# A second attention whose transposes and value products stand ahead of the look-ahead scores in every step

## The chip, the core and the metric

The program runs on one core of one Trainium2 chip, as a single launch. The metric is the device time of the whole program in microseconds (us); the number used for a kernel is the median of its runs.

## What is computed

The input is a sequence of 512 tokens of width 1024, in fp32. Block one is a gated linear recurrence (RG-LRU) with its projections, followed by an attention layer with a sliding window. Block two has a mixer of three attention families that share a sequence of "groups", and an MLP behind it. Cut to what the change touches:

```
stick:  z = q k^T * scale ; a = exp(log_sigmoid(z) + sum of log_sigmoid(-z) over later keys) ; o = a v   # 6 heads
cmp:    softmax over 31 compressed keys, 4 heads at once                                                # 4 heads
sel, win: softmax(q k^T * scale - slope * distance) v, causal                                           # 4 heads each
dil:    softmax over three key strips with stride 1, 4 and 16, merged by their sums                     # 2 heads
x = x + concat(o) @ w_out ;  x = x + relu(norm(x) @ w_up)^2 @ w_down
```

## The kernel before

The tokens are cut into 4 blocks of 128 (`n`). A **group** is one head of one kind with one query block `n`; its key width `w` is 128, 256, 384 or 512. The second attention (`make_attention(2)`) has 68 groups, numbered `i` from 0 to 67, in an order written out by hand: stick heads mixed with cmp, sel and win heads first, the dil heads between the last sel and win ones (constant `LATE`, 24 groups).

Each engine walks over the same step number `i` in its own queue, and semaphores tie the four queues together. In step `i`:

- **PE** (TensorE) issues `scores(i + 4)` (L769 and L772; L762 for cmp), `turn(i)` (the transposes of the probabilities of group `i`, L785) and `values(i - 1)` (the products with V of group `i - 1`, L805). After these stand, in some steps, `pair_turn` and `turn_chunk` (further transposes, L827: of a finished pair of heads, or of a dilated query or key, named ("q", m) or ("k", m)), and in 24 steps up to 29 a `piece`: 12 matmuls of a projection (L1298 to L1300). The pieces belong to three projections G1, G2 and G3, each with 4 token tiles of 2 pieces.
- **ACT** (ScalarE) takes the scores of a stick group in four passes (L878, L881, L883, L885) in step `i` for group `i + 3`, exponentiates masked scores (L904; L897 for cmp) and finishes stick probabilities (L921) for group `i + 2`, copies odd chunks of transposes out of PSUM (L926), and takes dilated chunks (L946, L947).
- **DVE** (VectorE) masks the scores of the other kinds (L1039; L1018 for cmp) for group `i + 3`, runs the running sum and the subtraction of stick groups (L1053, L1054) for `i + 2`, copies even chunks (L973), and scales finished heads (L1114, L1119).
- **POOL** (GpSimd) splits every weight unit into a high and a low part (L1248, L1250, L1251) ahead of the matmuls that use it. Four units fit into the ring, and a unit is split only when the matmuls with its predecessor in that slot are done (L1247 is the first instruction after that wait). Behind the units of G3 it prepares and splits the dilated queries and keys (L1209, L1219).

What a PE block waits for: `scores(i + 4)` waits until the score bank (three of them, four from group 36 on) has been read; `turn(i)` waits for the probabilities of `i`, and for its chunk bank. The chunks, numbered in PE's order, alternate between PSUM banks 3 and 4, so a chunk waits until the chunk two before it has been copied out. `values(i - 1)` waits for the copies of its chunks, and at the start of a head for the finished head before it in its output bank.

Whether the scores of a step go in front or behind was decided by a flag `late`. It was set for the scores of the last 24 groups, that is in steps 40 to 63:

```
late = a == 2 and ng - len(LATE) <= ahead < ng
if 0 <= ahead < ng and not late:
    scores(ahead)
...
if late:
    scores(ahead)
```

Of the kernel before, what the change touches and what calls it, by code (L numbers as in the profile page):

```python
# [153 lines left out]
LATE = "nnDnDnnDnDnnDnDnnDnDnnnn"  # L154
# [145 lines left out]
def two_block_kernel(nc, x_d, weights_d, params_d, tables_d, swa_d, ident_d, out_d):  # L300
    BANK, FREE, BEFORE, LAST_USE = plan()
    ctx = ExitStack()
    with ctx:
# [263 lines left out]
        def make_attention(a):  # L567
# [37 lines left out]
            def strip_read(st):  # L605

                return s[f"read{SB.index(strip_bank[st])}_"], strip_count[st]

            s = att[a]
            ng = len(groups)  # L610
# [130 lines left out]
            def pe_part(pe, item, tail, behind_scores=None):  # L741
# [33 lines left out]
                def turn(i):  # L775
                    g = groups[i]
                    if i == 0 and a == 2:
                        for k in (3, 4):
                            pe.wait_ge(FREESEM[LAST_USE[k][0]], LAST_USE[k][1])
                    pe.wait_ge(*probs_ready(i))  # L780
                    for c, blocks in g["chunks"]:
                        if c >= 2:
                            pe.wait_ge(s[("pt_even", "pt_odd")[c % 2]], c // 2)
                        for j, (strip, _, kb) in enumerate(blocks):
                            mm = pe.transpose(B[3 + c % 2][:, j * P:(j + 1) * P], probs_of(i, strip)[:, kb * P:(kb + 1) * P], ident[:])  # L785
                        mm.then_inc(s["pt_ready"], 1)

                def values(i):
                    g = groups[i]
                    b = g["b"]  # L790
                    kind = batches[b]["kind"]
                    if i == start_of[b]:
                        if ahead_in_bank(b) is not None:
                            pe.wait_ge(*fin_of(ahead_in_bank(b)))
                        elif a == 2:
                            pe.wait_ge(FREESEM[LAST_USE[bank_of[b]][0]], LAST_USE[bank_of[b]][1])
                        if kind in ("stick", "dil"):
                            pe.wait_ge(evac_a, FREE[("G4" if kind == "stick" else "G3", 3)][1])
                    out = out_cols(b, g["n"], 4 * HD if kind == "cmp" else VW)
                    first, total = True, sum(len(bl) for _, bl in g["chunks"])  # L800
                    for c, blocks in g["chunks"]:
                        pe.wait_ge(s[("pt_even", "pt_odd")[c % 2]], c // 2 + 1)
                        for j, (s_, _, kb) in enumerate(blocks):
                            total -= 1
                            mm = pe.matmul(out, pt[:, c % slots, j * P:(j + 1) * P], value_ap(g, s_, kb),  # L805
                                           start=first, stop=total == 0)
                            first = False
                    mm.then_inc(s["o_done"], 1)

                def pair_turn(p):  # L810
                    for b, batch in enumerate(batches):
                        if batch["pair"] == pair_of[p] and (batch["last"] or batch["kind"] == "dil"):
                            pe.wait_ge(*fin_of(b))
                    if a == 1 and before7[("pair", p)]:
                        pe.wait_ge(*before7[("pair", p)])
                    if a == 2:
                        turn_chunk(("pair", p), otok[:, slot[p]])
                        return
                    for t in range(TB):
                        mm = pe.transpose(B[7][:, t * P:(t + 1) * P], otok[:, slot[p], t, :], ident[:])  # L820
                    mm.then_inc(s["pairT"], 1)

                def turn_chunk(key, src):
                    c = chunk_of[key]
                    pe.wait_ge(*chunk_taken(c - 2))
                    for t in range(TB):
                        mm = pe.transpose(B[3 + c % 2][:, t * P:(t + 1) * P], src[:, t, :], ident[:])  # L827
                    mm.then_inc(s["pt_ready"], 1)

                for i in range(-LOOK - 1, ng + OUT_LAG):  # L830
                    ahead = i + LOOK + 1
                    late = a == 2 and ng - len(LATE) <= ahead < ng
                    if 0 <= ahead < ng and not late:
                        scores(ahead)
                    if i == -2 and a == 2:
                        behind_scores()
                    if 0 <= i < ng:
                        turn(i)
                    if 0 <= i - V_LAG < ng:
                        values(i - V_LAG)  # L840
                    if late:
                        scores(ahead)
                    if i - TURN_LAG in pairs:
                        pair_turn(pairs.index(i - TURN_LAG))
                    if a == 2 and i in TURNS2:
                        k = DIL_ORDER.index(TURNS2[i])
                        pe.wait_ge(dil_doubled, k + 1)
                        turn_chunk(TURNS2[i], doubles[k % 2])
                    if i in part_at:
                        key, q, parts = part_at[i]  # L850
                        if q == 0 and before7[key]:
                            pe.wait_ge(*before7[key])
                        item(key, range(KD * q // parts, KD * (q + 1) // parts))
                    if a == 2 and i in PIECES:
                        item(*PIECES[i])
                    for m, k0, k1 in TAILS[a].get(i - ng, ()):
                        if k0 > 0:
                            pass
                        elif m < 3:
                            pe.wait_ge(*strip_read(max(st for st, k in enumerate(strip_bank) if k == m)))  # L860
                        else:
                            pe.wait_ge(s["pt_even"], last_chunk // 2 + 1)
                        tail(m, range(k0, k1))
# [306 lines left out]
            def pool_part(pool):  # L1170
# [51 lines left out]
                for k in range(len(DIL_ORDER) + 1):  # L1222
                    if k < len(DIL_ORDER):
                        double(k)
                    if k > 0:
                        split_dil(k - 1)

            return pe_part, act_part, dve_part, len(pairs), lambda p: chunk_taken(chunk_of["pair", p]), pool_part

        def slope10(i):  # L1230
# [1256 lines left out]
```

## Time and profile before

| what | value |
|---|---|
| median of 3 runs | 1145.09 us |
| lowest, highest | 1144.65, 1145.69 us |
| the profiled execution's own time | 1148.06 us |
| span of its trace, first to last instruction | 1146.0 us |
| mean granted TensorE clock | 0.992 |
| PE, DVE, ACT, POOL busy | 96%, 54%, 38%, 46% of the span |

The second attention, from its first scores to its last value products, lies between 557.9 and 757.2 us of the span. The steps that the diff touches, 0 to 39, run from 568.39 us (`scores(4)`) to 693.09 us, where `turn(40)` starts. Steps were found in the trace by counting matmuls: a `turn` has one L785 for each 128 keys, a `values` has two L805 for each (fp32 data, two passes), and `scores` of a stick group three L769 and one L772, of sel and win two L769.

### The profile page before, as it was taken

The numbers are of one execution on the slowest core, as the hardware profiler recorded it, in microseconds if no ns is written. First come the engines' busy times: TensorE is split into PE (matmuls) and PEld (weight loads), VectorE is DVE, ScalarE is ACT, GpSimd is POOL, SyncE is SP. The second block draws the span as 40 slices with busy tenths as digits, with TensorE's granted clock in tenths as the row PEclk, the third lists the DMA queues.
The fourth block names the chain that finished last, engine by engine and source line by source line (L and its number), as shares of the span: only waits on it lengthen the run. The fifth ranks groups of instructions, "written<-read, shape, count | busy, mean of one in ns | idle before, by whom it ended". The sixth has DMA issues, their size and how long they took to land.

```text
span 1146.0 us, 16131 instructions
## 1 busy us (share of the span) xinstructions
PE 1101.0 (96%) x5801; PEld 940.1 (82%) x5801; DVE 619.3 (54%) x1102; ACT 435.5 (38%) x890; POOL 523.6 (46%) x521
## 2 busy tenths in 40 slices
PE   6999999999989999999999887999999999999998
PEld 5788888888869998888798886888878888888887
DVE  6869686668556763656655547856521321321321
ACT  5364758453335661213565578522110200210210
POOL 0000000000352434979833647229956776776772
PEclk9999999999999999999999989999999999999999
DMA  6332322313220101333311200103423222322221
GB/s 251 114 107 76 127 90 95 128 56 113 92 90 19 37 21 36 112 100 122 121 34 50 74 1 20 56 19 111 129 74 105 97 92 94 103 96 92 93 91 53
DMA packets 27279, 97.18 MB, mean 85 GB/s; under 512 B 3024, under 2 KB 3408, under 8 KB 27088
## 3 DMA queue, kind: packets, MB, share of 16 engines
q1 hardware_dynamic: 27216, 96.32, 25.1%
q8 instruction: 41, 0.67, 0.2%
q14 instruction: 22, 0.18, 0.0%
HBM read 94.21 MB, written 2.10 MB: 84 GB/s over the span
## 4 chain that ended last, share of the span: by engine, by line
PE 70%; DVE 9%; issue 8%; POOL 6%; ACT 6%; DMA 1%; POOLq 0%; SPq 0%; DVEq 0%; ACTq 0%
PE bank L1298 20%; PE bank L1300 20%; PE bank L1299 20%; PE bank L805 4%; PE bank L769 3%; POOL wl L1251 3%; PE bank L785 2%; POOL wh L1248 2%; DVE arena L2026 1%; DVE wl L1977 1%; ACT wh L1657 1%; POOL wl L1250 1%; DMA x<-x_in 1%; POOL hold L1247 1%; DVE arena L2361 0%
## 5 line engine op out<-in xcount | busy, mean ns | idle before, releaser
L1247 POOL TENSOR_TENSOR hold<-hold 128x2 f32<-128x2 f32 x117 | 29.9, 256 | 521.4 <-PE bank L1300 521.4
L1298 PE MATMUL bank<-xh,wh 128*128 128x512 f32 x568 | 227.1, 400 | 11.9 <-DVE xl L1946 9.8
L1299 PE MATMUL bank<-xl,wh 128*128 128x512 f32 x568 | 222.7, 392 | 0.0
L1300 PE MATMUL bank<-xh,wl 128*128 128x512 f32 x568 | 222.7, 392 | 0.0
L1298 PE MATMUL bank<-yh,wh 128*128 128x512 f32 x520 | 204.1, 393 | 2.9 <-DVE yl L2366 2.4
L1299 PE MATMUL bank<-yl,wh 128*128 128x512 f32 x520 | 203.0, 390 | 0.0
L1300 PE MATMUL bank<-yh,wl 128*128 128x512 f32 x520 | 203.0, 390 | 0.0
L1251 POOL TENSOR_TENSOR wl<-raw,wh 128x512 fp32r<-128x512 f32 x117 | 173.7, 1484 | 0.0
L1250 POOL TENSOR_TENSOR wl<-raw,wh 128x512 fp32r<-128x512 f32 x117 | 158.5, 1355 | 9.8
L1298 PEld LDWEIGHTS bank<-xh,wh 128*128 128x128 f32 x568 | 107.5, 189 | 35.2 <-issue 12.1
L1300 PEld LDWEIGHTS bank<-xh,wl 128*128 128x128 f32 x568 | 107.6, 189 | 22.8
L1248 POOL TENSOR_SCALAR wh<-raw 128x1024 fp32r<-128x1024 f32 x117 | 125.8, 1075 | 0.0
L1299 PEld LDWEIGHTS bank<-xl,wh 128*128 128x128 f32 x568 | 107.6, 189 | 21.6 <-issue 0.7
L1298 PEld LDWEIGHTS bank<-yh,wh 128*128 128x128 f32 x520 | 97.9, 188 | 24.7 <-DVE yl L2366 3.3
L1300 PEld LDWEIGHTS bank<-yh,wl 128*128 128x128 f32 x520 | 98.0, 189 | 20.6
L1299 PEld LDWEIGHTS bank<-yl,wh 128*128 128x128 f32 x520 | 98.1, 189 | 20.1
L1910 ACT ACTIVATE arena<-arena 128x512 f32<-128x512 f32 x32 | 20.3, 633 | 246.4 <-DVE arena L2361 246.4
L2373 DVE TENSOR_TENSOR x<-bank,x 128x512 f32<-128x512 f32 x32 | 22.1, 692 | 142.4 <-PE bank L1300 142.4
L805 PE MATMUL bank<-arena 128*128 128x64 f32 (+1 forms) x620 | 87.3, 270 | 3.2 <-ACT arena L926 2.4
L1977 DVE TENSOR_TENSOR wl<-raw,wh 128x1024 fp32r<-128x1024 f32 x56 | 68.0, 1222 | 39.8 <-ACT wh L1657 39.4
L1298 PE MATMUL bank<-wh,xh 128*128 128x512 f32 (+2 forms) x224 | 84.3, 376 | 4.1 <-POOL wl L1251 3.0
L805 PEld LDWEIGHTS bank<-arena 128*128 128x128 f32 x620 | 82.0, 196 | 6.0 <-ACT arena L926 2.9
(258 smaller groups left out, 1801.0 us busy)
## 6 DMA issues: line engine op xcount, KB each, us to landing
raw<-weight_units SPq DMA_DIRECT2D x173, 512.0 KB, 3.5
x<-x_in SPq DMA_DIRECT2D x4, 512.0 KB, 8.0
out_fm<-x SPq DMA_DIRECT2D x8, 256.0 KB, 2.0
arena<-tables SPq DMA_DIRECT2D x1, 1024.0 KB, 10.3
par<-params SPq DMA_DIRECT2D x1, 166.0 KB, 2.3
arena<-swa_table SPq DMA_DIRECT2D x1, 128.0 KB, 11.1
ident<-identity SPq DMA_DIRECT2D x1, 64.0 KB, 8.3
```

Of the source, the lines that this page charges most:

```text
L769: mm = pe.matmul(out, q, kk, start=t == 0, stop=t == len(terms) - 1 and kind != "stick")
L785: mm = pe.transpose(B[3 + c % 2][:, j * P:(j + 1) * P], probs_of(i, strip)[:, kb * P:(kb + 1) * P], ident[:])
L805: mm = pe.matmul(out, pt[:, c % slots, j * P:(j + 1) * P], value_ap(g, s_, kb), start=first, stop=total == 0)
L1247: pool.tensor_tensor(hold[:], hold[:], hold[:], ALU.add).then_inc(held, 1)
L1248: pool.tensor_scalar(wh[:, j, :], raw[:, j, :], 1.0, 1.0, ALU.mult, ALU.mult).then_inc(high_done, 1)
L1250: pool.tensor_tensor(wl[:, j, 0:512], raw[:, j, 0:512], wh[:, j, 0:512], ALU.subtract)
L1251: pool.tensor_tensor(wl[:, j, 512:1024], raw[:, j, 512:1024], wh[:, j, 512:1024], ALU.subtract)\
L1298: pe.matmul(out, lh, rh, start=start, stop=False)
L1299: pe.matmul(out, lh, rl, start=False, stop=False)
L1300: return pe.matmul(out, ll, rh, start=False, stop=stop)
L1977: dve.tensor_tensor(wl[:, u % RING, :], raw[:, u % RING, :], wh[:, u % RING, :], ALU.subtract)\
L2373: dve.tensor_tensor(x[:, m, :], B[4 + m % 4][:], x[:, m, :], ALU.add).then_inc(down_read, 1)
```

## The change

The flag is now set in every step from 0 on. In steps 0 to 39 the scores, those of groups 4 to 43, move behind `turn(i)` and `values(i - 1)`. They stay ahead of `pair_turn`, of `turn_chunk` and of the piece. Steps 40 to 63 had this order already. Nothing is added or taken out, and no other queue changes.

```
--- before.py
+++ after.py
@@ -829,7 +829,7 @@
 
                 for i in range(-LOOK - 1, ng + OUT_LAG):
                     ahead = i + LOOK + 1
-                    late = a == 2 and ng - len(LATE) <= ahead < ng
+                    late = a == 2 and 0 <= i and ahead < ng
                     if 0 <= ahead < ng and not late:
                         scores(ahead)
                     if i == -2 and a == 2:
```

## Rows read from the trace of the kernel before

**Rows 1.** First line of the page.

```profile
span 1146.0 us, 16131 instructions
```

**Rows 2.** Stages: start:end length, then PE, PEld, DVE, ACT, POOL busy; clock, DMA, GB/s.

```profile
568.40:592.20 23.80, 23.64 (x158) 23.37 (x159) 15.21 (x43) 18.36 (x53) 2.38 (x3) 1.00 0.08 24
592.20:608.80 16.60, 14.90 (x105) 14.12 (x103) 9.50 (x38) 10.20 (x43) 16.18 (x16) 1.00 0.29 95
608.80:626.60 17.80, 16.93 (x107) 16.29 (x108) 9.17 (x26) 10.00 (x28) 0.02 (x1) 1.00 0.10 32
626.60:643.70 17.10, 14.14 (x94) 12.71 (x92) 11.16 (x22) 8.25 (x22) 16.77 (x17) 1.00 0.28 92
643.70:667.40 23.70, 23.67 (x149) 23.34 (x150) 7.34 (x24) 10.12 (x29) 4.17 (x10) 0.93 0.07 23
667.40:693.10 25.70, 20.04 (x133) 18.17 (x132) 14.74 (x34) 22.37 (x56) 16.82 (x14) 0.87 0.00 1
693.10:757.40 64.30, 56.95 (x451) 52.22 (x449) 47.76 (x146) 38.83 (x114) 25.09 (x25) 1.00 0.11 34
```

**Rows 3.** Waits in 520 to 660 us: total, times, longest.

```profile
POOL hold L1247 <- PE bank L1300: 40.0, 3, 21.4
```

**Rows 4.** PE by line and form, 568.4 to 693.1 us; behind the bar its idle time.

```profile
L805 PE MATMUL bank<-arena 128*128 128x64 f32 x168 | 24.6, 278 | 2.4 <-ACT arena L926 2.0 <-DVE arena L1119 0.3
L1298 PE MATMUL bank<-wh,xh 128*128 128x384 f32 x64 | 23.7, 371 | 3.9 <-POOL wl L1251 3.0 <-ACT arena L1888 0.9
...
L785 PE MATMUL bank<-ident,arena 128*128 128x128 f32 x91 | 18.6, 298 | 2.7 <-ACT arena L947 2.0 <-DVE yl L1144 0.7
```

**Rows 5.** PE's timeline in steps 12, 30 and 39: start, duration; idle in brackets.

```profile
606.22 0.66 PE L805 MATMUL bank<-arena 128*128 128x64 f32 x4 [1.30 <-ACT arena L926]
...
667.25 0.39 PE L769 MATMUL bank<-yh 128*128 128x512 f32 x1
...
667.95 0.22 PE L772 MATMUL bank<-yh 128*128 128x128 f32 x1
668.91 0.30 PE L785 MATMUL bank<-ident,arena 128*128 128x128 f32 x1 [0.75 <-ACT arena L947]
669.59 0.66 PE L805 MATMUL bank<-arena 128*128 128x64 f32 x4 [0.37 <-ACT arena L926]
670.08 1.05 PE L827 MATMUL bank<-ident,arena 128*128 128x128 f32 x8
...
689.13 0.48 PE L769 MATMUL bank<-yh 128*128 128x512 f32 x1
...
691.37 0.41 PE L785 MATMUL bank<-ident,arena 128*128 128x128 f32 x2 [1.24 <-ACT arena L947]
692.15 0.66 PE L805 MATMUL bank<-arena 128*128 128x64 f32 x4 [0.37 <-ACT arena L926]
692.64 0.61 PE L827 MATMUL bank<-ident,arena 128*128 128x128 f32 x4
```

**Rows 6.** POOL's timeline in step 12: the last unit of G2.

```profile
606.78 1.94 POOL L1251 TENSOR_TENSOR wl<-raw,wh 128x512 fp32r<-128x512 f32 x1
```

**Rows 7.** ACT's timeline in its steps 31, 37 and 40.

```profile
670.29 0.61 ACT L878 ACTIVATE arena<-bank 128x512 f32<-128x512 f32 x1
...
686.12 0.42 ACT L921 ACTIVATE arena<-arena 128x256 f32<-128x256 f32 x1 [1.36 <-DVE arena L1054]
...
692.40 0.60 ACT L878 ACTIVATE arena<-bank 128x512 f32<-128x512 f32 x1
```

**Rows 8.** Short stretches, the columns of rows 2.

```profile
640.40:643.80 3.40, 1.39 (x9) 1.07 (x8) 3.33 (x5) 0.42 (x1) 3.40 (x3) 1.00 0.35 134
671.20:674.60 3.40, 1.70 (x13) 1.23 (x12) 2.74 (x5) 3.37 (x9) 0.83 (x2) 1.00 0.00 0
674.60:681.40 6.80, 6.80 (x36) 6.80 (x35) 2.45 (x8) 5.50 (x15) 5.19 (x5) 0.50 0.00 1
688.30:691.70 3.40, 2.16 (x14) 1.54 (x12) 2.16 (x4) 3.37 (x9) 2.20 (x3) 1.00 0.00 0
```

More of the change, by code:

```diff
@@ L831, in pe_part @@
                     ahead = i + LOOK + 1
-                    late = a == 2 and ng - len(LATE) <= ahead < ng
+                    late = a == 2 and 0 <= i and ahead < ng
                     if 0 <= ahead < ng and not late:
```

## The prediction

> **What bounds the kernel now.** I read the page first, for the span [rows 1], then cut the second attention into stages, at the places where a different engine sets the pace, and asked for busy times and clock stage by stage [rows 2]. Then I read the waits, PE's idle time by line, and the timelines of PE, ACT, DVE and POOL step by step.
>
> The reader is to see four kinds of stage in [rows 2]. In 568.4 to 592.2 and in 643.7 to 667.4 PE is busy to the end: 23.64 of 23.80 us and 23.67 of 23.70. In 592.2 to 608.8 and in 626.6 to 643.7 it is POOL, 16.18 of 16.60 and 16.77 of 17.10 us: it splits four weight units, and can't begin before PE has finished the pieces that hold the ring (three waits, 40.0 us, the longest 21.4 [rows 3]). The stage between them is PE's again (16.93 of 17.80). In 667.4 to 693.1 PE is busy for only 20.04 of 25.70 us and ACT for 22.37: the pieces are used up, and ACT has the dilated chunks on top of its work. Only here do PE's transposes wait for a chunk bank that ACT or DVE has not read yet (2.7 us in all [rows 4]). After 693.1 us the order is the new one already, PE is busy for 56.95 of 64.30 us and DVE for 47.76; nobody has much slack, so what arrives late there ends late.
>
> **The change part by part.** Steps 0 to 39 issue the same blocks; 40 score blocks move behind a `turn` and a `values`. No DMA, no instruction of another queue and no wait moves with them, and the pieces stand behind all three blocks in both orders. So PE's work up to each piece is the same, and the change can act only in two ways: transposes and value products come earlier by the length of a score block (0.3 to 1.0 us), and scores come later by the length of a `turn` and a `values`, plus whatever these wait for.
>
> *The stages that PE or POOL bounds: 568.4 to 667.4 us.* In the 30 steps up to 29 I compared, for every step, when the probabilities and copies were ready with when PE would now want them. Probabilities are ready over 1.2 us before the step starts in all of them. The scores are read by ACT or DVE 0.04 to 4.4 us after they end, so some readers (groups 14, 22, 25, 29) will start later by 0.3 to 0.8 us. What hides it is the piece that PE computes behind, or POOL's split. Value: nothing. Its one exposed place is step 12. Before, `values(11)` waits 1.30 us there for ACT's copy, until 606.22 [rows 5], and POOL finishes the last unit of G2 at 606.78 + 1.94 = 608.72 us [rows 6], which the second half of the next piece needs. Now `scores(14)` comes some 0.45 us later, ACT's four passes and the copy behind it as well, and `scores(16)` (0.92 us, below) follows `values(11)`. The second half then starts some 0.9 us after POOL is done. But the piece behind it waits for ACT (L1888), 0.9 us before [rows 4], and ACT is held there by DVE's sum, which doesn't move. So the wait takes up the delay, and I keep 0.1 us. Ends: 0 and 0.9. At step 0 `scores(4)` waits for its bank in either order; `turn(0)` slips into that wait, worth under 0.1 us.
>
> *Step 30.* This is the first place where the old order filled a wait. `scores(34)` ran from 667.25 to 667.95 + 0.22 = 668.17, so 0.92 us, while `turn(30)` waited until 668.91 for the bank that ACT's L947 reads, and `values(29)` until 669.59 for a copy [rows 5]. Both waits are ACT's, and do not get shorter. In the new order `scores(34)` starts where the block behind `values(29)` starts now, at 670.08, and ends at 671.00. ACT wanted these scores at 670.29 [rows 7]. So ACT, the busiest engine of this stage, idles for 0.7 us, and four passes, the taking of the next dilated chunk and the next chunk's turn on PE follow 0.7 us later. Part of it is given back in steps 34 to 37. There ACT waits 1.36 us for DVE's L1054, until 686.12 [rows 7], and DVE had waited for `values(34)`, which is now ahead of `scores(39)`, about 0.3 us earlier. I take back 0.2. Term: 0.5 us. Ends: 0 and 0.7.
>
> *Step 39.* The same pattern, and longer. Before, `scores(43)` started at 689.13, inside the wait of `turn(39)`, which could start only at 691.37 after 1.24 us idle; `values(38)` then waited for a copy until 692.15, and the next block came at 692.64 [rows 5]. ACT took the scores at 692.40, right behind its preceding pass [rows 7]. In the new order they start at 692.64 and end 0.92 us later, at 693.56. ACT idles for 693.56 - 692.40 = 1.2 us. In the chain that ended last ACT's passes from 692.4 on, its take of ("q", 3), then POOL and DVE follow without a gap, so I count all of it. Ends: 0, if DVE or POOL would have held up what follows anyway, and 1.2.
>
> *Steps 31 to 38 otherwise.* The other score blocks moved here are wanted 0.35 to 3.3 us after they ended, and the `values` ahead of them mostly don't wait. `scores(38)` becomes late for ACT by about 0.4 us, but ACT then waits for DVE (the same 1.36 us). Nothing.
>
> Sum: 0.1 + 0.5 + 1.2 = 1.8 us. The profiled execution (1148.06 us, 2.1 above its span) would become 1149.9, and the median of the runs, 3.0 below it, 1145.09 + 1.8 = 1146.9 us.
>
> *The clock.* The granted clock fell from 1.00 to 0.50 (from 2.4 to 1.2 GHz) after 3.4 us in which PE was busy for 1.39 us, and again after 3.4 us with 1.70 busy; after 688.3 to 691.7, with 2.16, it stayed at 1.00 [rows 8]. In the new order `scores(43)` (0.92 us) leaves this last stretch, and PE is busy for about 1.2 us there, less than in either stretch ahead of a fall. The other two falls stay where they are, since POOL's and ACT's waits that lead to them stay.
>
> The Trainium skill (TensorE: Matmul & The Clock Gate, Part 4: PE-mode transpose) says that transposes don't count as PE being busy in the way other matmuls do. By that rule what is left in the stretch counts for even less than its 1.2 us, and the time would be that of the low-clock rival below, 1148.2, rather than 1146.9; by the rows alone both are open. The trace has transposes in all four stretches and can't separate them.
>
> **The rivals.**
>
> *One more stretch at the low clock, after 691.7 us (the slower side).* For: the busy times just compared. Against: the stretch at 688.3 begins with work of the step before, and where PE's pause lies against the clock's decisions can shift by a few us. Price: from 674.6 to 681.4 PE was busy for all 6.80 us at 0.50 [rows 8], so 3.4 us of low clock hold 1.7 us of work at full clock. Of what PE does behind 692.1 only `values(38)`, `scores(43)` and the short blocks of steps 40 and 41 are on the path, some three quarters: 1.3 us. Time: 1146.9 + 1.3 = 1148.2. It decides from the moment PE pauses for most of some 3 us behind `scores(42)`. Two such stretches in a row would give 1149.5.
>
> *The delay is absorbed behind step 40.* DVE is busy for 47.76 of 64.30 us there [rows 2], and if it or POOL's dilated splits set the pace, ACT's 1.2 us at step 39 is hidden. Against it speaks the chain, which goes through ACT's passes of group 43. Left is 0 to 0.5 us: 1145.4.
>
> *The earlier transposes gain more than the later scores lose.* PE waits 2.4 us for copies ahead of `values` in these steps [rows 4]. 1.3 of it is step 12, which POOL covers. If the other 1.1 us went, because copies start earlier by a score block, and ACT's gaps at steps 30 and 39 didn't show, the time would be 1145.09 - 1.1 = 1144.0. Against: the copies at steps 29 and 38 are late because ACT is busy, not because their transposes are.
>
> **How the numbers follow.** Chances: 0.40 for the sum (its own range 1146.0 to 1148.0), 0.30 for the low-clock stretch (1147.2 to 1149.5), 0.18 for absorbed (1145.0 to 1145.8), 0.12 for the gain (1143.0 to 1144.8). Predicted is 1146.9. The range that holds 8 in 10 leaves out the lower part of the gain and the upper of the low clock: 1144.1 to 1149.0. A change of 0.2% is 2.3 us, about what a measurement of this kernel can tell from none: faster needs under 1142.8, which only the edge of the last case reaches: 0.04. Slower needs over 1147.4: most of the low-clock case (0.26) and the upper end of the sum (0.10): 0.36. Within: 0.60.
>
> **What would show it.** At the end of the pieces (667.4 us before) the two traces should be level within 0.3 us. In step 30 `turn(30)` and `values(29)` should follow with the same waits, `scores(34)` behind them, and ACT's L878 should show an idle time on PE's L772 of about 0.7 us. In step 39 the same with 1.2 us or more. The lag at `turn(40)` should be 1.5 to 2 us and stay up to the tail tiles. Wrong would be: a lag before 660 us (POOL fed later at G2 or G3), a lag that melts behind 700 us, or a low-clock stretch that comes or goes.

## The result and the profile after: 0.8% slower

| | before | after |
|---|---|---|
| median (lowest to highest) | 1145.09 (1143.59 to 1145.69), 5 runs | 1154.30 us (1151.36 to 1159.04), 5 runs |
| ratio, 95% interval | | 1.0079 [1.0059, 1.0099] |
| profiled execution, its span | 1148.06, 1146.0 us | 1151.83, 1149.8 us |
| mean granted clock in it | 0.992 | 0.988 |

Run again later, 12 times beside 35 runs of the kernel before, it gave 1152.23 us and 1.0047 [1.0027, 1.0067] (experiment 11). The loss is 6 to 9 us, where 1.8 was predicted; it lies outside the range.

The first line of the page, and the row of its 40 slices with the granted clock in tenths:

```profile
span 1149.8 us, 16131 instructions
...
PEclk9999999999999999999999987999999999999999
```

The dip is in slices 24 and 25, 661 to 719 us, where steps 29 to 48 lie. A count of matmuls finds `turn(i)` in both traces, and the difference of its starts shows where time was lost (us; positive is late). Up to step 39 `turn(i)` stands one score block further forward than before, so -0.2 to -1.0 is level there; from step 40 on the two orders are the same:

| block | before | after | difference |
|---|---|---|---|
| `turn(10)` | 602.64 | 602.05 | -0.6 |
| `values(11)` | 606.22 | 606.70 | +0.5 |
| `turn(14)` | 614.36 | 613.85 | -0.5 |
| `turn(23)` | 639.33 | 638.62 | -0.7 |
| `turn(25)` | 650.31 | 648.21 | -2.1 |
| `turn(33)` | 676.67 | 676.23 | -0.4 |
| `turn(39)` | 691.37 | 691.37 | 0.0 |
| `turn(40)` | 693.09 | 695.40 | +2.3 |
| `turn(42)` | 698.04 | 701.58 | +3.5 |
| `turn(43)` | 700.26 | 705.76 | +5.5 |
| `turn(47)` | 708.24 | 714.64 | +6.4 |
| L827, step 72 | 760.89 | 767.41 | +6.5 |

From step 1 to 23 all turns but that of step 13 lie between -0.1 and -1.1 us: level. The 1.5 us or so won at steps 24 to 29 are the clock's: in before it was at 0.50 from 643.9 to 647.3 us, in this execution of after it was not. They are gone again by step 33. `turn(39)`, which waits for ACT, starts at the same time in both. 2.3 us arise in step 39, and 4.1 more from step 40 to 47. At the end of the span 3.8 of the 6.5 are left: the lag drops between 830 and 853 us, where before has one more low stretch, 841.9 to 845.3, far behind the attention.

The level `turn(39)` hides a loss. ACT's queue is the same in both kernels, so its own instructions show the lag without a shift of order. The L947 that `turn(30)` waits for starts at 668.09 us before and 666.52 after, the one that `turn(39)` waits for at 690.55 and 690.54. So after enters step 30 ahead by 1.6 us and has lost all of it by step 39.

The stages that answer to the last two of [rows 2] (the same steps), then the stretch ahead of the fall at step 39, and the whole low stretch behind it:

```profile
667.20:695.60 28.40, 22.83 (x132) 20.02 (x133) 14.66 (x32) 21.71 (x55) 17.51 (x14) 0.80 0.00 1
695.60:764.00 68.40, 62.02 (x450) 57.59 (x449) 46.80 (x147) 38.92 (x114) 25.19 (x24) 0.91 0.10 32
...
687.40:690.80 3.40, 1.73 (x10) 1.11 (x10) 1.40 (x5) 3.37 (x10) 2.32 (x2) 1.00 0.00 0
...
690.80:707.90 17.10, 15.48 (x69) 14.66 (x70) 9.12 (x23) 10.55 (x24) 8.43 (x7) 0.50 0.01 1
```

For the last row, a stretch of before as long as it, over about the same steps:

```profile
688.30:705.40 17.10, 12.87 (x102) 11.41 (x101) 13.42 (x33) 15.77 (x40) 12.35 (x11) 1.00 0.01 1
```

In 17.1 us before has 102 matmuls and PE is idle for a quarter of it; after has 69 and PE is idle for 1.6 us. At 1.2 GHz PE has become the bound of a stage in which it had waited for others: ACT's busy time falls from 15.77 to 10.55.

PE's timeline at steps 30 and 39, to be held against [rows 5] (idle time in brackets):

```profile
667.35 0.30 PE L785 MATMUL bank<-ident,arena 128*128 128x128 f32 x1 [1.51 <-ACT arena L947]
668.02 0.66 PE L805 MATMUL bank<-arena 128*128 128x64 f32 x4 [0.37 <-ACT arena L926]
668.49 0.48 PE L769 MATMUL bank<-yh 128*128 128x512 f32 x1
...
691.37 0.66 PE L785 MATMUL bank<-ident,arena 128*128 128x128 f32 x2 [1.78 <-ACT arena L947]
692.14 1.12 PE L805 MATMUL bank<-arena 128*128 128x64 f32 x4
693.02 0.77 PE L769 MATMUL bank<-yh 128*128 128x512 f32 x1
...
694.44 0.31 PE L772 MATMUL bank<-yh 128*128 128x128 f32 x1
694.55 1.05 PE L827 MATMUL bank<-ident,arena 128*128 128x128 f32 x4
```

Both pauses grew, 0.75 to 1.51 us and 1.24 to 1.78, the first by most and the second by over half of the 0.92 us that the score block had filled. At step 30 the block behind them is as long as before, 0.48 us for its first matmul. At step 39 the clock has fallen inside the pause (690.8), and everything behind it takes 1.6 to 1.7 times as long: 0.77 against 0.48, 1.12 against 0.66. ACT's timeline shows what that makes of the scores it waits for:

```profile
669.52 0.60 ACT L878 ACTIVATE arena<-bank 128x512 f32<-128x512 f32 x1 [0.67 <-PE bank L772]
...
692.08 0.53 ACT L921 ACTIVATE arena<-arena 128x384 f32<-128x384 f32 x1
694.79 0.60 ACT L878 ACTIVATE arena<-bank 128x512 f32<-128x512 f32 x1 [2.18 <-PE bank L772]
```

0.67 us at step 30, where the prediction had 0.7, and 2.18 at step 39, where it had 1.2. Between them ACT waits twice more where it did not before, the second time for scores:

```profile
676.14 0.63 ACT L921 ACTIVATE arena<-arena 128x512 f32<-128x512 f32 x1 [0.74 <-DVE arena L1054]
...
681.69 0.38 ACT L878 ACTIVATE arena<-bank 128x256 f32<-128x256 f32 x1 [0.62 <-PE bank L772]
```

The pause that grew most is in step 12, among the steps that the prediction held for free. It was 1.30 us in [rows 5]:

```profile
606.70 0.66 PE L805 MATMUL bank<-arena 128*128 128x64 f32 x4 [2.61 <-ACT arena L926]
```

It costs no time by itself here (the table above), and in this execution the clock stayed at 1.00 behind it.

PE's idle time by line in these 40 steps, and the waits for the ring, answer to [rows 4] and [rows 3]:

```profile
L805 PE MATMUL bank<-arena 128*128 128x64 f32 x168 | 24.6, 279 | 4.5 <-ACT arena L926 4.4
L1298 PE MATMUL bank<-wh,xh 128*128 128x384 f32 x64 | 22.5, 352 | 2.0 <-POOL wl L1251 1.8 <-ACT arena L1888 0.2
...
L785 PE MATMUL bank<-ident,arena 128*128 128x128 f32 x90 | 18.1, 296 | 5.4 <-ACT arena L947 4.0 <-DVE yl L1144 1.2 <-ACT arena L926 0.2
```

```profile
POOL hold L1247 <- PE bank L1300: 40.6, 3, 21.6
```

POOL's waits are as before. What transposes and value products wait for grew from 5.1 to 9.9 us, what the first matmuls of pieces wait for fell from 3.9 to 2.0. Waits that score blocks had filled are now idle time.

### The profile page after: what moved, and what is told of

The parts are those of the page before. It is cut to its first block, busy times and chain, and to the rows that moved or that the text cites. A ratio compares the mean times of both kernels' runs of the same rounds, so it can differ in the third digit from the quotient of the medians.

```text
span 1149.8 us, 16131 instructions
## 1 busy us (share of the span) xinstructions
PE 1105.0 (96%) x5801; PEld 944.3 (82%) x5801; DVE 618.7 (54%) x1102; ACT 436.2 (38%) x890; POOL 525.6 (46%) x521
## 4 chain that ended last, share of the span: by engine, by line
PE 71%; DVE 9%; issue 8%; ACT 6%; POOL 5%; DMA 1%; POOLq 0%; SPq 0%; DVEq 0%; ACTq 0%
PE bank L1298 20%; PE bank L1300 20%; PE bank L1299 20%; PE bank L805 4%; PE bank L769 3%; POOL wl L1251 2%; PE bank L785 2%; POOL wh L1248 2%; DVE arena L2026 1%; DVE wl L1977 1%; POOL wl L1250 1%; ACT wh L1657 1%; DMA x<-x_in 1%; PE bank L827 0%; DVE arena L2361 0%
## 5 line engine op out<-in xcount | busy, mean ns | idle before, releaser
L1298 PEld LDWEIGHTS bank<-xh,wh 128*128 128x128 f32 x568 | 107.6, 189 | 35.0 <-issue 11.8
L805 PEld LDWEIGHTS bank<-arena 128*128 128x128 f32 x620 | 84.5, 201 | 8.6 <-ACT arena L926 4.1
```

The lines of the kernel that those rows point to most:

```text
L1298: pe.matmul(out, lh, rh, start=start, stop=False)
```

## Experiments

Two theories were set against each other. **Lateness**: each score block that ACT or DVE needs at once arrives later, and the delays add up. **Clock**: PE's longer pause lets the granted clock fall more often or for longer, and at half clock PE sets the pace.

The clock varies from run to run, so each run's mean granted clock was turned into a time at low clock, L = 2 x (1 - clock) x span, good to some 1.2 us, since the clock is recorded to three decimals. All kernels of a batch ran on one chip beside before. The medians and ratios are the comparison's. The means leave out two runs of before in batch one: one of 2205.6 us, and one of 1152.14 us with a mean clock of 0.94 (L = 136). They keep one run of experiment 4 that is as odd, 1146.86 us with L = 48.1; without it, its mean L is 14.4.

| kernel | new order in steps | median us | ratio, 95% | mean us | mean L, us |
|---|---|---|---|---|---|
| before, three batches | none | 1144.73, 1145.26, 1145.72 | | 1144.6, 1145.3, 1145.8 | 12.6, 13.4, 14.4 |
| after (first) | 0 to 39 | 1154.30 | 1.0079 [1.0059, 1.0099] | 1154.5 | 29.1 |
| 1 | 30 to 39 | 1147.21 | 1.0025 [1.0010, 1.0040] | 1147.8 | 18.5 |
| 2 | 0 to 29 | 1143.98 | 0.9992 [0.9976, 1.0008] | 1144.0 | 10.5 |
| 3 | 39 | 1150.06 | 1.0034 [1.0014, 1.0054] | 1148.4 | 21.8 |
| 4 | all but 39 | 1146.78 | 1.0015 [1.0000, 1.0030] | 1146.9 | 17.2 |
| 5 | all, filler in 39 | 1150.43 | 1.0044 [1.0027, 1.0061] | 1150.0 | 18.9 |
| 6 | none, pause in 39 | 1149.52 | 1.0031 [1.0016, 1.0045] | 1149.1 | 27.5 |
| 7 | all but 30, 39 | 1146.86 | 1.0008 [0.9993, 1.0023] | 1146.4 | 15.1 |
| 8 | none, three fillers | 1144.68 | 1.0003 [0.9987, 1.0020] | 1145.3 | 11.1 |
| 9 | 0 to 29, three fillers | 1145.49 | 0.9997 [0.9976, 1.0018] | 1145.8 | 11.8 |
| 10 | all, three fillers | 1147.90 | 1.0010 [0.9992, 1.0028] | 1148.1 | 11.3 |
| 11 | all (after again) | 1152.23 | 1.0047 [1.0027, 1.0067] | 1151.8 | 25.9 |
| 12 | all but 30, 39, three fillers | 1148.41 | 1.0024 [1.0009, 1.0039] | 1148.2 | 16.6 |

Experiments 1 to 4 are batch one, 5 to 8 two, 9 to 12 three.

### 1 to 4: which steps

```diff
-late = a == 2 and 0 <= i and ahead < ng
+late = a == 2 and 30 <= i and ahead < ng                      # 1
+late = a == 2 and (0 <= i < 30 or 40 <= i) and ahead < ng     # 2
+late = a == 2 and 39 <= i and ahead < ng                      # 3
+late = a == 2 and 0 <= i and i != 39 and ahead < ng           # 4
```

> Scores behind only from step 30 on; steps 0 to 29 as before. Clock theory (the order at step 39 leaves a pause of PE that sets off a stretch at 1.2 GHz, and PE is then the bound): as slow as the change, 1151 to 1159 us, with low clock from about 691 us on. Rival, late scores only: 1145.1 + 1.8 = 1146.9 us. Rival, the early steps carry the loss: within 1 us of before.

> Scores behind in steps 0 to 29 and from 40 on; steps 30 to 39 as before. Clock theory and late-scores rival alike: within 1 us of before, 1144 to 1146 us, and no low clock behind 690 us. Rival, the early steps carry the loss: 1149 us or more.

> Only step 39 is added to the steps that have scores behind. Clock theory: most of the loss of the change, 1150 us or more, and a low-clock stretch from about 691 us on in the trace. Rival, late scores only: ACT's idle time of 1.2 us at group 43, 1146.3 us. Rival, the loss is spread over the steps: under 1146 us.

> The whole change without step 39, so that scores of group 43 stand in front of turn 39. Clock theory: no stretch of low clock behind 690 us, 1145 to 1146.5 us. Rival, late scores only: 0.6 us more than before, 1145.7 us, so the same reading. Rival, the loss is spread over the steps: 1149 us or more.

Steps 0 to 29 are free by themselves: 1143.98 against 1144.73 us, an interval that holds 1. All of the loss needs steps 30 to 39. Step 39 alone costs 3.8 us in the mean, all the others without it 2.3; together 6.1, of the 6 to 9 of the full change. Cut at step 30 instead, the parts do not add up: 3.2 and -0.6. Not all of this is what the clock theory expected: experiment 1 came out at 1147.21 us, far from its 1151 and at the rival's 1146.9, and experiment 2 has low clock behind 690 us in its profile, from 711.8 to 718.6 us. Experiments 3 and 4 lie at the edges of the clock theory's ranges.

Experiment 3 is the telling one, since its runs lie so far apart: 1142.24 and 1142.31 us with L of 9.1 and 6.8, then, past four in between, six runs from 1150.4 to 1151.5 us with L = 27.6. One order of instructions, 8 us apart. Its profile is of the run at 1142.24; here the stretch ahead of the fall at step 39, the fall, and what follows:

```profile
681.60:685.00 3.40, 1.48 (x10) 1.24 (x10) 2.06 (x8) 3.37 (x10) 2.34 (x2) 1.00 0.00 0
685.00:691.80 6.80, 5.81 (x23) 5.09 (x23) 2.53 (x5) 4.48 (x11) 2.32 (x2) 0.50 0.00 0
691.80:708.90 17.10, 14.02 (x111) 12.64 (x110) 14.86 (x44) 14.35 (x41) 13.04 (x12) 1.00 0.01 2
```

Even here the clock falls in step 39's pause and ACT idles, for 2.29 us. But it is back after 6.8 us, and there is no other low stretch until 1139.0 us, where PE has finished. So the lateness is in the kernel's fastest run too; what the longer runs have more is low clock.

One place of the fall follows the order in every profile. Scores of group 43 are gone from ahead of `turn(39)`, with nothing in their place, in experiments 1, 3 and 6 and in both profiles of after: in all five the clock falls in the pause of step 39. In the other nine profiles it does not, with `scores(43)` or a filler ahead of `turn(39)`.

### 5 and 8: filling the pause

Experiment 5 is after with a second, unsignalled copy of `scores(43)` ahead of `turn(39)`; its operands are ready, and the real one overwrites it. Experiment 8 is before with four 512-column matmuls of ready data, into the bank that the next scores will fill, in the pauses of steps 31, 37 and 39.

```diff
+if a == 2 and i == 39:            # 5
+    scores(ahead, False)
```

```diff
+if a == 2 and i == 39:            # 8; also at i in (31, 37), behind values
+    filler(44, 4)
```

> The change, plus one thing: in step 39 the matmuls of the scores of group 43 are issued a first time ahead of turn 39, without a signal, where the kernel before had them; the real ones follow behind values 38. The pause is filled, the scores are as late as in the change. Clock theory: the low clock behind 690 us goes in most runs, and with it most of the loss: 1146 to 1149 us, spread of the runs under 4 us. Late scores: nothing changes against the change, 1154 us.

> The kernel before with 4 matmuls of 512 columns (0.9 us) put into each of three of PE's waits: ahead of the turns of (q, 4) in step 31 and (q, 1) in step 37, and ahead of turn 39. Their results are overwritten. Clock theory: fewer us of low clock than before and a time 1 to 3 us lower, 1142 to 1144. If the clock hardly costs time here: 1144.7 or up to 1 us more.

Filling step 39's pause alone takes L from the 26 to 29 us of after to 18.9, and 2 to 4 us off after's two medians. That is less than was expected: the median of 1150.43 us lies above the 1146 to 1149 of the clock theory, and the nine runs spread over 8.2 us, not under 4. In its profile the clock holds through step 39, ACT idles there for 1.06 us, and `turn(39)` still waits 1.03 us for ACT behind the filler, so the filler delays nothing; low clock comes at 561.1, 677.2 and 701.1 us instead. 4.8 us above before stay in the mean, of which the 5.5 us of low clock more explain 2.0 to 2.8 by the slopes under experiments 10 and 11. In before the three fillers take L from 13.4 to 11.1 and change nothing in the time, where 1 to 3 us were expected: the scatter of its runs, 1142.6 to 1151.0, is no smaller.

### 6: the pause without lateness

Before, but `scores(42)` and `scores(43)` are issued at the end of step 37, and none in steps 38 and 39. No score is later, and PE has nothing to fill the waits with.

```diff
-if 0 <= ahead < ng and not late:
+if 0 <= ahead < ng and not late and not (a == 2 and i in (38, 39)):
...
+if a == 2 and i == 37:
+    scores(42)
+    scores(43)
```

> The kernel before, but the scores of groups 42 and 43 are issued at the end of step 37, ahead of the turn of (q, 1), and no longer in steps 38 and 39. No score is late; PE's pause in step 39 holds 1.4 us less work. Clock theory: a stretch of low clock from about 691 us in most runs, 1148 us or more. Late scores: no loss, 1144 to 1145.5 us.

It costs 1149.52 against 1145.26 us, with L = 27.5, as in after. Its lines stand 3 lower in the code (L947 is L950). PE's timeline at step 39, ACT's, and the two stretches:

```profile
689.91 0.66 PE L785 MATMUL bank<-ident,arena 128*128 128x128 f32 x2 [2.30 <-ACT arena L950]
690.69 1.12 PE L805 MATMUL bank<-arena 128*128 128x64 f32 x4
691.60 1.06 PE L827 MATMUL bank<-ident,arena 128*128 128x128 f32 x4
```

```profile
690.52 0.53 ACT L924 ACTIVATE arena<-arena 128x384 f32<-128x384 f32 x1
690.93 0.60 ACT L881 ACTIVATE arena<-bank 128x512 f32<-128x512 f32 x1
```

```profile
686.40:689.80 3.40, 1.19 (x8) 0.84 (x8) 2.06 (x6) 3.37 (x10) 2.23 (x2) 1.00 0.00 0
689.80:703.50 13.70, 13.45 (x62) 12.92 (x63) 9.03 (x22) 9.45 (x21) 8.02 (x7) 0.50 0.01 2
```

ACT takes the scores of group 43 without any idle time, and still 13.7 us of low clock begin in the pause. This is the experiment that tells the theories apart: the pause alone, without a late score, brings L to that of after and costs 3.9 us in the mean. The only run with L = 13.7 took 1144.35 us, no more than before.

### 7, 9 and 12: can the rest of the change be kept

```diff
+late = a == 2 and 0 <= i and i not in (30, 39) and ahead < ng   # 7; 12 with the fillers
```

Experiment 9 is 2 with the fillers of 8.

> The change without steps 30 and 39. If the late scores of group 34 are what the kernel without step 39 alone still loses (1146.8 against 1144.7 us), this is 0.5 to 1.5 us faster than it, 1145 to 1146 us. If its loss comes from the other steps between 31 and 38, it stays at 1146.8.

> The new order in steps 0 to 29 and 40 to 63, the old in 30 to 39, and four 512-column filler matmuls of ready data in each of the three pauses of PE at steps 31, 37 and 39. If the two halves are independent (the order of steps 0 to 29 neutral, the fillers worth what they take away of the low clock), the time is 1142.5 to 1144.5 us, and it beats both kernels by a hair. If the fillers only displace the low clock, it is the time of the kernel before, 1145.1, or more.

> The new order in all steps but 30 and 39, with the same three fillers. If steps 31 to 38 cost nothing by themselves and only the clock stood in the way: 1143 to 1145 us, as the one of steps 0 to 29 with fillers. If the scores that stand late in steps 31 to 38 still delay ACT: 1 to 2 us more than that one at equal low clock.

None beats before: 7 and 9 are level with it, 12 is 2.7 us slower, with L of 16.6, no less than the 15.1 of experiment 7 without fillers. Experiment 7 is at experiment 4's time, 1146.86 and 1146.78 us, so group 34's late scores are not what 4 loses. Experiment 12 met neither of its two expectations: it is 2.4 us above 9 in the mean, but with 4.8 us more low clock, which by the slopes below is worth 1.8 to 2.4. In its profile PE pauses once more, ahead of the dilated turn of step 40, for 1.85 us, and the clock falls at the end of that pause, from 694.6 to 698.0; the profile of 7 has the same pause, 1.85 us, and the same fall. But the profile of 2 has this pause as well, 1.76 us, and keeps its clock: such a pause can set off a fall and need not. The pauses come from ACT, and filling one leaves the next.

### 10 and 11: how much is each

Experiment 10 is after with the three fillers, 11 is after itself.

> The changed kernel with the same three fillers. If its loss is above all low clock that PE's pauses set off, low-clock time per execution falls from about 29 us to under 15 and the time from 1154 to 1147 or 1148; what is left over before, 2 to 3 us, is then the lateness of the scores (the 1.8 us of the prediction). If the loss is lateness that adds up over the steps, it stays above 1152 though the clock is better.

> The changed kernel itself, beside the kernel before on the same chip, for the scatter of time against low-clock time. Clock theory: 1152 to 1156 us, and among its executions those with least low clock (under 17 us) lie within 3 us of the kernel before, those with most 8 us or more above, a slope of some 0.5 to 0.9 us of time for each us of low clock. Lateness theory: all lie 6 us or more above before whatever their clock.

In 10, the clock is at 1.00 through step 39. PE's and ACT's timeline there (fillers are L782, and lines behind them stand 9 to 13 lower: L785 is L794, L878 is L891), and a stretch around it:

```profile
696.56 1.09 PE L782 MATMUL bank<-yh 128*128 128x512 f32 x4
698.51 0.41 PE L794 MATMUL bank<-ident,arena 128*128 128x128 f32 x2 [0.86 <-ACT arena L960]
699.29 0.66 PE L814 MATMUL bank<-arena 128*128 128x64 f32 x4 [0.37 <-ACT arena L939]
699.75 0.48 PE L769 MATMUL bank<-yh 128*128 128x512 f32 x1
```

```profile
700.80 0.60 ACT L891 ACTIVATE arena<-bank 128x512 f32<-128x512 f32 x1 [1.06 <-PE bank L772]
```

```profile
690.00:710.00 20.00, 15.79 (x116) 13.64 (x116) 14.71 (x33) 15.89 (x37) 12.75 (x11) 1.00 0.01 1
```

ACT idles for 1.06 us at full clock, against 2.18 at half. (This profile is of the kernel's longest run, 1155.98 us; its low clock, 27.7 us, lies in other places.) The mean time, 1148.1 us, stands against 1145.8 of experiment 9 on the same chip, with the same fillers and nearly the same L (11.3 and 11.8). So 2.3 us is an estimate of what the order of steps 30 to 39 costs when the clock is even. The runs of each kernel have a standard deviation of over 3 us, so this difference has a 95% interval of 2.6 us either way. The traces give about the same: 1.6 us lost from step 30 to 38 in the first profile of after (1.3 in the second, by the same L947), and 1.06 at step 39.

For the clock's part I took all runs of the two batches of after (17) and of the three of before (100, without the two named above; with the one of 1152.14 us the slope below would be 0.09 and not 0.37, so the line holds for the usual low clock and not for that run's). Means: 1152.6 us at L = 26.8, and 1145.2 at 13.5. A straight line through before's runs has a slope of 0.37 us for each us of low clock, through after's 0.50. So 13.3 us more of low clock are worth 4.9 to 6.7 us, and with the 2.3 above this is 7.2 to 9.0, where the means are 7.3 apart. The two runs of after with least low clock (13.7 us) took 1146.17 and 1146.23 us; 28 runs of before with as much have a median of 1145.5. By these two the lateness is 0.7 us and not 2.3; so the share of lateness is known only as some 1 to 2 us.

In 11's profile the fall comes in the same pause, but ends sooner:

```profile
691.50:694.90 3.40, 1.88 (x12) 1.11 (x10) 1.35 (x6) 3.37 (x10) 2.34 (x3) 1.00 0.00 0
694.90:701.80 6.90, 5.93 (x23) 5.09 (x23) 2.76 (x5) 4.68 (x11) 2.32 (x2) 0.51 0.00 0
```

There the lag grows by 2.3 us from `turn(39)` to `turn(40)`, as in the first profile of after, and by only 0.2 from there to `turn(47)` (4.1 in the first). This separates the step itself from the length of the low stretch behind it.

## Why the prediction was wrong, step by step

- *568.4 to 667.4 us worth nothing.* Right as a sum. The steps are level but for the clock's stretch, and experiment 2 is at 0.9992. The delay at step 12 went as described: `values(11)` came 0.5 us later, and at step 14 nothing of it was left. What was overlooked is that the old order filled a wait here already, not first at step 30: `scores(16)` stood in it, and PE's pause grew from 1.30 to 2.61 us. In the profiles of the nine kernels with the new order at step 12 it is 2.6 us, and the clock falls there in four of them (4, 9, 10 and 11); in none of the five with the old order. Step 30 begins at 667.25 before (`scores(34)`) and at 667.35 after (`turn(30)`).
- *Step 30, ACT idles for 0.7 us, 0.5 after what comes back.* The idle time is right, 0.67. But it was not given back, and steps 31 to 38 were not worth nothing: ACT waited 0.74 and 0.62 us more in them, and got 0.9 us back where it waits for DVE's L1054 (1.36 before, 0.46 after). By ACT's L947 steps 30 to 38 cost 1.6 us where the sum had 0.5; `turn(39)` is level only because after came in 1.6 us ahead.
- *Step 39, 1.2 us.* The mechanism is right, and at full clock so is the size: 1.06 us in experiment 10. In after it measured 2.18, and 2.3 at `turn(40)`, because the block I costed at 0.92 us runs at half clock (693.02 to 694.75, 1.7 us), behind value products that do too. The lateness of the whole change, by 10 against 9, is 2.3 us where the sum had 1.8, and the wide interval holds both.
- *The clock: the step that failed.* The likeliest case let the clock be, and the rival priced "one more stretch" at 1.3 us for 3.4 us of low clock, 2.6 for two. The place and the cause were right: PE pauses behind `scores(42)`, busy for 1.73 of 3.40 us, against 2.16 in [rows 8], and the clock falls there in both profiles of after. The size was not. The low stretch lasted 17.1 us in one profile and 6.9 in the other, and over 17 runs a run has 13.3 us more of it, four times the one stretch that I priced; its share is 4.9 us or more of the 7.3. The price of each us of low clock, 1.3 / 3.4 = 0.38, was about right: 0.37 over before's runs and 0.50 over after's. So what failed was to take the length of a low stretch for that of one of the shortest shown, though 674.6 to 681.4 in [rows 8] was already twice as long, and to hold the fall for less likely than not.
- *The Trainium skill's rule, that transposes don't count as PE being busy in the way other matmuls do* (TensorE: Matmul & The Clock Gate, Part 4: PE-mode transpose), pointed to the low-clock rival, and the traces went that way: of the 1.73 busy us ahead of the fall, 1.04 are L785's and L827's transposes. But the prediction misread its rows: 640.4 to 643.8 holds no transposes at all, and the clock fell behind its 1.39 busy us; 688.3 to 691.7 has 1.29 us besides 0.87 of transposes, and it stayed. So leaving the transposes out does not sort these stretches. Nor does the total: at step 12 of after PE was busy for 0.79 of 3.40 us (603.3 to 606.7), and the clock stayed at 1.00. No run here took the transposes away, so the rule stays untested.
- *Absorbed* and *earlier transposes gain*: neither. The lag stays at 6.5 us up to step 72, and PE's waits for copies ahead of `values` grew from 2.4 to 4.5 us.

What stays open: why a pause is followed by low clock in one execution and not in another; why the low stretch is at one time 6.9 and at another 17.1 us long with the same instructions in the same pause; and why steps 0 to 29, free by themselves, are needed for the full loss (1 and 2 give 2.6 us together). Their pause at step 12 may have a part in it; no run here filled it.

## What to carry to other kernels

A block with ready operands ahead of a wait is a filler: where another engine is the bound, moving it behind the wait takes nothing off that engine, makes the block late by its own length, and empties PE. Find the longest pauses of PE in the trace, ask what runs in them, and leave that there. In the 30 of 40 steps where PE itself or POOL's split set the pace, the same order cost nothing by itself. When a change makes a pause longer next to places where the clock has already fallen, price the low clock by at least the longest low stretch of the trace, not the shortest (here that is 6.8 us, still half of the 13.3 that came), and expect the runs to scatter: compare at least ten, and set each one's time against its clock.

## What the runs showed of the hardware

One kernel's time scatters with its clock. Experiment 3 took 1142.24 to 1151.53 us with 6.8 to 27.6 us at low clock; after took 1146.17 to 1159.04 with 13.7 to 34.7.

A full PE does not at once bring the clock back. Three stretches of the low clock in after (the columns of rows 2):

```profile
701.00:704.40 3.40, 3.40 (x18) 3.40 (x18) 2.43 (x5) 1.24 (x4) 2.93 (x3) 0.50 0.01 2
704.40:707.80 3.40, 3.40 (x19) 3.40 (x18) 1.39 (x9) 1.80 (x5) 0.45 (x1) 0.50 0.00 0
677.20:680.60 3.40, 3.40 (x18) 3.40 (x18) 1.65 (x6) 2.11 (x6) 1.49 (x2) 0.50 0.00 0
```

PE is busy to the end in all three. Behind the last of them the clock rose, at 680.6; behind the first it did not, at 704.4. With the transposes' share left out the first has 2.34 us and the last 1.27, so that does not sort them either.
